# One sample tile of an input projection, dealt over four column groups of the matmul array

## The chip, the cores and the metric

The kernel runs on one core of one Trainium2 chip. The metric is the device time of one execution in microseconds (us). Three timed runs of the kernel before have a median of 1442.5 us.

## The reference, cut to what matters

One step of a streaming encoder layer, for a prompt of 1024 positions and a sample of 32 positions that follow a cache of 1024. Both go through the same weights. What the change touches is the first product, the normalised input times one wide weight matrix whose columns are split among the users:

```
PROJ_SIZES = (ATTN_WIDTH, ATTN_WIDTH, ATTN_WIDTH, N_IDX_HEADS * IDX_DIM, IDX_DIM, N_IDX_HEADS, SGU_WIDTH, SGU_WIDTH)
...
xn = _rms_norm(x, g_attn)
q, k, v, qi, ki, wi, u, vs = _mixer_inputs(xn, w_in, pos)      # jnp.split(xn @ w_in, ...), rotary on q, k, qi, ki
# qi, ki, wi: index scores, the 256 best keys of each query;  q, k, v: attention over those keys
# vs: gelu, normalised over groups of 128, mixed over 128 positions;  u: gelu, times the mixed vs
h = x + concat(attention, u * mixed) @ w_out
y = h + (silu(hn @ w_gate) * (hn @ w_up)) @ w_down
```

D_MODEL is 1024. The widths are 512, but for ki (64) and wi (8).

## The kernel before, in words

The 1056 rows are cut into nine tiles of 128, t = 0 to 8. Tile 8 (LAST) is the sample: its 32 rows (DEC) stand in the tile four times (PACK), loaded by four DMAs, so that all later steps find 128 rows. The matrix w_in is taken in seven chunks of columns, c = 0 to 6: qi, ki (with wi, 72 columns), vs, u, k, v, q, in this order. Every chunk but ki has 512 columns. The loop is over chunks, inside it over tiles, and each engine has its own written order for it (the function `step` in each engine's block); semaphores tie the orders together.

A float32 product is made of f16 parts: input and weight are each split into a high and a low part, and three products are summed (high x high, high x low, low x high). For one tile of one chunk, `main` on TensorE (L901, matmuls at L913) runs KT = 8 blocks of the 1024 times these three, 24 matmuls of up to 512 columns with a 128 x 128 stationary operand, into PSUM bank 2 or 3 (`par(c, t)` alternates).

What follows for each tile:

- ScalarE, `E` (L1279): empties the bank into the buffer e32 (for v: into r32 and V; for vs: through a Gelu with sums, four instructions at L1295).
- GpSimd, `A` (L705): rotary (L731 to L736) or, for u, a multiplication (L716), into r32. `B` (L738): subtraction that makes the low half (L763). In a tile's step GpSimd does A of this tile and then B of the tile before. For vs it has `vs_means` (L779), `vs_stats` (L768 to L774) and `vs_affine` (L784, L786).
- ScalarE, `H` (L1333, for vs L1314): cast to f16, the high half. `vs_squares` (L1362) and `vs_normalise` (L1371) for vs.
- TensorE, `post` (L946, L950): transposes of the two halves, called turns below, 8 at a time, two tiles late. In q there are two sets of turns a tile, the second after `dup_q` on ScalarE (L1347).
- ScalarE, `R` (L1392): empties the turns, two tiles late; `ST` (L1411): issues the store of k, v and ki rows.

A tile's `main` may start when E of two tiles before is done. ScalarE also splits the next chunk's weights (`piece_hi`, L436) in steps 0 and 1 of a chunk. From chunk u on, each step also holds one round of a binary search for the 256th best score: VectorE counts five score tiles (L1815), ScalarE two (`sign_count`, L1451, and L1455), VectorE judges (L1821) and sets the next bit (L1827). VectorE has 31 such rounds; the last is in tile 3 of q. Before that, in vs, the index scores are made (TensorE L972, ScalarE L1422, VectorE L1778 and L1781). After q, attention begins (TensorE L1039, VectorE L1923), then the output projection and the feed-forward.

In the output projection the sample's tile is already dealt over four column groups (L1138): each group of 32 columns of the array gets two of the eight blocks, and VectorE adds the four parts.

Of the kernel before, what the change touches and what calls it, by code (L numbers as in the profile page):

```python
# [36 lines left out]
P = 128  # L37
# [63 lines left out]
def encoder_step(nc, a):  # L101

    ctx = ExitStack()
    with ctx:
        M = ctx.enter_context(nc.sbuf_tensor("M", [P, 209600 // 4], F32))

        def sem(name):
            return ctx.enter_context(nc.semaphore(name))
# [120 lines left out]
        PS = ctx.enter_context(nc.psum_tensor("PS", [P, 8, 512], F32))  # L229
        PSf = PS[:, :, :].rearrange("p a b -> p (a b)")  # L230
        sign_out = view(RS, 8192, [TOK], F16)
        kth = cand.bitcast(F32)

        def bank(b):
# [19 lines left out]
        ws_turned, ws_hi, ws_lo, ws_ready = sem("ws_turned"), sem("ws_hi"), sem("ws_lo"), sem("ws_ready")  # L254
        kic_hi, kic_ready = sem("kic_hi"), sem("kic_ready")
        main_done, evac_done = sem("main_done"), sem("evac_done")
        rope_mul, r_ready = sem("rope_mul"), sem("r_ready")
        cast_done, sub_done, dup_done = sem("cast_done"), sem("sub_done"), sem("dup_done")
        post_done, post_evac = sem("post_done"), sem("post_evac")
# [60 lines left out]
            return FIRST_UNITS + before(c, lambda n: UNITS[n]) + UNITS[NAMES[c]] * t  # L320

        cC = {n: i for i, n in enumerate(NAMES)}

        def par(c, t):
            return (c + t) % 2
# [339 lines left out]
        def _(pool):  # L665
# [23 lines left out]

            x_rms(0, 0)  # L690
            x_rms(1, 1)
            pool.dma_start(ws32, a["w_s"][0].rearrange("g i j -> i g j")).then_inc(ws_loaded, 16)

            pool.wait_ge(kic_hi, 1)
# [194 lines left out]
        def _(pe):  # L889
# [11 lines left out]
            def main(c, t, rep):  # L901
                w = CHUNKS[c][2]
                b = 2 + par(c, rep)
                if c == 0:
                    pe.wait_ge(x_lo, t + 1)
                if c or not isinstance(t, int) or t >= 2:
                    pe.wait_ge(evac_done, n_step(c, t) - 1)
                for k in range(KT):
                    if isinstance(t, int) and t == 0 and k % pieces[first_piece[c]][2] == 0:
                        pe.wait_ge(w_split, first_piece[c] + k // pieces[first_piece[c]][2] + 1)  # L910
                    terms = ((0, wh), (0, wl), (1, wh))
                    for i, (s, wt) in enumerate(terms):
                        last = pe.matmul(bank(b)[:, 0:w], xnT[:, ds(t, 1), k, s, :].squeeze(1),  # L913
                                         wt[wbuf(c)][:, k * w:(k + 1) * w],
                                         start=(k == 0 and i == 0), stop=(k == KT - 1 and i == 2))
                last.then_inc(main_done, 1)

            def spatial(c, t, rep):
                pe.wait_ge(sub_done, n_cast(cC["vs"], t) + 1)
# [62 lines left out]
            for c in range(NC):  # L982
                def step(t, rep, c=c):
                    if c == 0 and isinstance(t, int) and t == 0:
                        main(c, t, rep)
                        X(1, 1)
                        return
                    if c == 0 and t_below(t, rep, LAST):
                        X(t + 1, rep + 1)
                    if c == 0 and isinstance(t, int) and t == 1:  # L990

                        pe.wait_ge(kic_ready, 1)
                        for s in range(2):
                            for i in range(8):
                                last = pe.transpose(bank16(4 + s)[:, i, :], dump[s][:, i * P:(i + 1) * P],
                                                    ident16[:])
                            last.then_inc(post_done, 1)
                        pe.wait_ge(ws_loaded, 16)
                        for g in range(GROUPS):
                            last = pe.transpose(bank(7)[:, g * P:(g + 1) * P], ws32[:, g, :], ident[:])  # L1000
                        last.then_inc(ws_turned, 1)
                    if NAMES[c] == "u":
                        if isinstance(t, int) and t == 0:
                            pe.wait_ge(ws_ready, 1)
                            pe.wait_ge(score_relu, NS * HEADS)
                        spatial(c, t, rep)
                    main(c, t, rep)
                    if NAMES[c] == "vs":
                        if t == 0:
                            flush(post, c - 1, 2)  # L1010
                        if t < NS:
                            score_products(t)
                    else:
                        lagged(post, c, t, rep, 2)
                steps(pe, c, step, *(LOOP[c] if c != 1 else (NT, NT)))
            flush(post, NC - 1, 2)

# [239 lines left out]
        def _(act):  # L1257
# [18 lines left out]
            act.wait_ge(kic_loaded, 16)  # L1276
            act.activation(kic2[0], kic32.unsqueeze(2).broadcast_to([P, 8, 2, HD]), ACT.Copy).then_inc(kic_hi, 1)

            def E(c, t, rep):  # L1279

                name, w, p = NAMES[c], CHUNKS[c][2], par(c, rep)
# [175 lines left out]
            for c in range(NC):  # L1457
                def step(t, rep, c=c):
                    if c == 0:
                        if t_below(t, rep, LAST):  # L1460
                            x_cast(t + 1, rep + 1)
                        if t_below(t, rep, LAST - 1):
                            x_square(t + 2, rep)
                    if NAMES[c] != "vs":
                        next_pieces(c, t)
                    lagged(dup_q, c, t, rep, 2)
                    E(c, t, rep)
                    if searching(c, t):
                        sign_count(c, t, 0)
                    if NAMES[c] == "vs":  # L1470
                        if t < NS:
                            score_relus(t)
                        vs_squares(c, t, rep)
                        next_pieces(c, t)
                    lagged(only_vs(H), c, t, rep, 2)
                    lagged(only_vs(ST), c, t, rep, 2)
                    lagged(only_vs(vs_normalise), c, t, rep, 1)
                    lagged(not_vs(H), c, t, rep, 1)
                    lagged(not_vs(ST), c, t, rep, 1)
                    if NAMES[c] == "u":  # L1480
                        sgu_evac(c, t, rep)
                    if isinstance(t, int) and t == 1 and NAMES[c] == "k":
                        act.wait_ge(score_acc, 2 * NS * HEADS)
                    lagged(R, c, t, rep, 2)
                    if searching(c, t):
                        sign_count(c, t, 1)
                    if c == 0 and isinstance(t, int) and t == 1:
                        for s in range(2):
                            act.wait_ge(post_done, s + 1)
                            act.activation(kiTs[:, s, :], PS[:, 4 + s, :].bitcast(F16),  # L1490
                                           ACT.Copy).then_inc(post_evac, 1)
                        act.wait_ge(ws_turned, 1)
                        act.activation(wmT[:, 0], bank(7).rearrange("p (g n) -> p g n", g=GROUPS), ACT.Copy,
                                       scale=WS).then_inc(ws_hi, 1)
# [724 lines left out]
```

## Time and profile before

| what | value |
|---|---|
| median of three runs (1441.97 to 1443.82) | 1442.5 us |
| the profiled execution | 1444.24 us |
| its span, first to last instruction | 1442.4 us |
| TensorE matmul busy | 1288.1 us (89%) |
| VectorE busy | 811.7 us (56%) |
| ScalarE busy | 716.7 us (50%) |
| GpSimd busy | 495.9 us (34%) |
| mean granted TensorE clock | 0.958 |

The times of instructions are from one profiled execution. Its span is counted from the first instruction, and all instants below are microseconds from there. TensorE is PE in the rows, its weight loads PEld, VectorE DVE, ScalarE ACT, GpSimd POOL. A row of a timeline has the start, the length, the engine, the line, the operation, what it writes and reads, and in brackets how long the engine had been idle before and what released it. TensorE's matmuls overlap, so a run of them is shorter than their number times the length of one. A granted clock of 1.00 is 2.4 GHz, 0.50 is 1.2 GHz.

### The profile page before, as it was taken

What the parts mean: (1) busy time and instruction counts of PE and PEld (TensorE: products, weight loads), DVE (VectorE), ACT (ScalarE), POOL (GpSimd) and SP (SyncE); (2) the same over time, 40 slices, a digit from 0 to 9 for tenths busy, and PEclk for the clock granted to TensorE, in tenths of its full rate; (3) what the DMA queues carried; (4) which work ended last, traced back from release to release, by engine and by line L of the source; (5) the groups of instructions that cost most, each with busy time, mean ns of one, the idle gap of its engine ahead of it and who ended that gap; (6) DMA issues with size and microseconds to landing.
All of it is one profiled execution on the core that took longest, in us unless ns stands there. A gap on an engine that the chain in (4) does not pass through costs nothing.

```text
span 1442.4 us, 29500 instructions
## 1 busy us (share of the span) xinstructions
PE 1288.1 (89%) x10636; PEld 927.3 (64%) x10636; DVE 811.7 (56%) x1495; ACT 716.7 (50%) x1408; POOL 495.9 (34%) x543
## 2 busy tenths in 40 slices
PE   4977788999996676798997999999999998999997
PEld 2443333544443445565455888888888887888886
DVE  4323675889889575896656555566555552212022
ACT  4546888787784844893434444444444441001011
POOL 4772436368258531442003333333333300000001
PEclk9989999999999579999998999999999999999999
DMA  6221001212100310114231222112222137211013
GB/s 196 89 61 35 15 1 46 59 37 82 65 17 0 87 38 16 45 31 140 88 103 41 63 58 58 43 45 58 58 58 58 29 90 206 62 63 37 0 30 91
DMA packets 81596, 86.69 MB, mean 60 GB/s; under 512 B 6768, under 2 KB 63120, under 8 KB 81520
## 3 DMA queue, kind: packets, MB, share of 16 engines
q1 hardware_dynamic: 76112, 75.07, 18.2%
q10 hardware_dynamic: 4848, 8.99, 1.7%
q0 software_dynamic: 560, 1.61, 0.4%
q8 instruction: 49, 0.80, 0.2%
q14 instruction: 27, 0.22, 0.0%
HBM read 72.34 MB, written 13.31 MB: 59 GB/s over the span
## 4 chain that ended last, share of the span: by engine, by line
PE 54%; DVE 5%; ACT 4%; issue 2%; POOL 2%; DMA 1%; SPq 1%; POOLq 0%; ACTq 0%; DVEq 0%
PE PS L1182 29%; PE PS L1239 15%; PE PS L1145 5%; DVE M L1934 1%; PE PS L1062 1%; PE PS L1039 1%; PE PS L1092 1%; DVE M L1923 1%; DMA M<-in_w_down 1%; ACT M L1524 1%; ACT M L1513 1%; SPq L647 1%; PE PS L1226 1%; PE PS L1159 0%; DMA M<-in_g_ffn 0%
## 5 line engine op out<-in xcount | busy, mean ns | idle before, releaser
L1182 PE MATMUL PS<-M 128*128 128x264 f16 x3696 | 420.8, 278 | 9.6 <-ACT M L1628 9.6
L1182 PEld LDWEIGHTS PS<-M 128*128 128x128 f16 x3696 | 363.3, 98 | 66.5 <-ACT M L1628 10.2
L913 PE MATMUL PS<-M 128*128 128x512 f16 (+1 forms) x1512 | 305.8, 363 | 3.6 <-DVE M L442 3.6
L1239 PE MATMUL PS<-M 128*128 128x256 f16 x2112 | 233.3, 274 | 6.3 <-DVE M L2148 6.3
L913 PEld LDWEIGHTS PS<-M 128*128 128x128 f16 (+1 forms) x1512 | 138.5, 103 | 153.9 <-issue 13.6
L1239 PEld LDWEIGHTS PS<-M 128*128 (+1 forms) x2112 | 207.2, 98 | 32.1 <-issue 7.3
L1815 DVE TENSOR_SCALAR_CACHE_REDUCE M<-M,small 128x384 f16<-128x384 f32 (+5 forms) x162 | 132.9, 881 | 0.8
L861 POOL TENSOR_TENSOR M<-M 128x264 f32<-128x264 f32 x44 | 34.7, 790 | 283.2 <-ACT M L1628 283.2
L683 POOL TENSOR_TENSOR small<-small 128x1 f32<-128x1 f32 x27 | 5.5, 203 | 331.5 <-ACT M L1720 237.2
L1987 DVE SCALAR_TENSOR_TENSOR M<-M 128x2048 f16<-128x2048 f32 (+1 forms) x44 | 88.9, 2025 | 36.1 <-ACT M L1566 36.1
L2148 DVE SCALAR_TENSOR_TENSOR M<-PS,M 128x256 f32 (+1 forms) x32 | 13.6, 424 | 165.5 <-PE PS L1239 165.4
L1628 ACT ACTIVATE M<-PS 128x264 f32<-128x264 f32 x132 | 51.2, 388 | 100.8 <-PE PS L1182 87.8
L1145 PE MATMUL PS<-M 128*128 128x512 f16 x384 | 84.2, 379 | 0.0
L1651 ACT ACTIVATE M<-M 128x1024 f16<-128x1024 f32 (+1 forms) x24 | 22.7, 978 | 116.8 <-PE PS L1226 82.3
L1451 ACT ACTIVATE M<-M,small 128x1056 f16<-128x1056 f32 x62 | 72.8, 1175 | 9.8 <-DVE small L1827 8.9
L1566 ACT ACTIVATE M<-M 128x2048 f16<-128x2048 f32 (+1 forms) x44 | 74.2, 1688 | 0.1
L1638 ACT ACTIVATE M<-M 128x264 f32 (+1 forms) x88 | 37.2, 423 | 70.2 <-DVE M L2072 36.2
L1062 PE MATMUL PS<-ident,M 128*128 128x128 f32 x306 | 56.5, 297 | 16.8 <-DVE M L1934 10.3
L1934 DVE TENSOR_TENSOR M<-PS,M 128x512 f16<-128x512 f32 (+3 forms) x102 | 53.4, 548 | 29.4 <-ACT M L1524 28.7
L2064 DVE TENSOR_TENSOR M<-PS,M 128x264 f32<-128x264 f32 x44 | 18.9, 431 | 83.8 <-PE PS L1182 82.3
L1145 PEld LDWEIGHTS PS<-M 128*128 128x128 f16 x384 | 37.5, 98 | 43.5
L1524 ACT ACTIVATE M<-PS 128x512 f16<-128x512 f32 (+3 forms) x102 | 47.9, 486 | 31.8 <-PE PS L1062 20.0
(177 smaller groups left out, 1943.0 us busy)
## 6 DMA issues: line engine op xcount, KB each, us to landing
M<-in_w_in SPq DMA_DIRECT2D x24, 512.0 KB, 3.7
M<-in_w_gate SPq DMA_DIRECT2D x22, 512.0 KB, 4.1
M<-in_w_up SPq DMA_DIRECT2D x22, 512.0 KB, 5.2
M<-in_w_down SPq DMA_DIRECT2D x20, 512.0 KB, 4.1
M<-in_x_prompt SPq DMA_DIRECT2D x16, 512.0 KB, 4.8
M<-in_w_out SPq DMA_DIRECT2D x8, 512.0 KB, 3.9
h_scratch<-M ACTq DMA_DIRECT2D x8, 512.0 KB, 5.1
M<-h_scratch SPq DMA_DIRECT2D x16, 256.0 KB, 7.3
```

The lines of the kernel that those rows point to most:

```text
L913: last = pe.matmul(bank(b)[:, 0:w], xnT[:, ds(t, 1), k, s, :].squeeze(1), wt[wbuf(c)][:, k * w:(k + 1) * w], start=(k == 0 and i == 0), st ...
L1062: last = pe.transpose(bank(pt_bank(g))[:, i * P:(i + 1) * P], LP[j % 4][:, (b0 + i) * P:(b0 + i + 1) * P], ident[:])
L1145: last = pe.matmul(bank(2 * p + d), mixT[:, t, k, s, :], wt[d][:, k * 512:(k + 1) * 512], start=(k == 0 and i == 0), stop=(k == KT - 1 and ...
L1182: last = pe.matmul(o, wsp[x][:, zw, wb, k * P:(k + 1) * P], ablk[:, ab, za, k * HT + s * SC:k * HT + (s + 1) * SC], start=(name not in kep ...
L1239: last = pe.matmul(o[:, 0:256], cols[:, ds(m * SC + r * P, P)], wt[dc % 2][:, f, :], start=(f == 0 and i == 0), stop=(f == FT - 1 and i == 2))
L1451: act.activation(sign_out, scores[:, o:o + TOK], ACT.Sign, scale=-1.0, bias=kth[:, j:j + 1], accum_out=signs[:, i:i + 1]).then_inc(signs_s ...
L1524: act.activation(PTs[pv_count[g] % 3][:, 0, 0:x * P], bank(pt_bank(g))[:, 0:x * P], ACT.Copy).then_inc(pt_hi, 1)
L1566: act.activation(wsp[x][:, 0, 4 * half:7 if half else 4, :], tb if half else raw[x], ACT.Copy, scale=WS).then_inc(w2_hi, 1)
L1628: act.activation(buf[s], bank(BANKS[x][s]["a"])[:, 0:SC], ACT.Copy).then_inc(kept, 1)
L1815: dve.tensor_scalar(dump[x][:, 0:S], scores[:, o:o + S], kth[:, j:j + 1], None, ALU.is_ge, ALU.add, accum_out=cnt[:, j:j + 1]).then_inc(se ...
L1934: dve.tensor_tensor(r[:, 1, 0:x * P], bank(pt_bank(g))[:, 0:x * P], r[:, 0, 0:x * P], ALU.subtract).then_inc(pt_ready, 1)
L1987: dve.scalar_tensor_tensor(out=wsp[x][:, 1, b, :], in0=tb if half else raw[x], scalar=WS, in1=wsp[x][:, 0, b, :], op0=ALU.mult, op1=ALU.su ...
```

## The change

In the six chunks of 512 columns, tile 8 is no longer a full product. Each of the four column groups of the array gets 32 columns of the stationary operand (the sample's rows once) and two of the eight blocks, so that 24 matmuls of 128 x 32 by 512 leave four partial sums of the 32 rows in the four quarters of the bank's partitions. ScalarE copies the bank into e32 (r32 for v). One f32 matmul with a 128 x 128 matrix of zeros and ones (`fold`, four times four identities of 32 x 32) adds the four parts and writes the sum to all four quarters, into the same bank. E then empties it as before.

`fold` is made once by GpSimd, by four copies after the second tile's statistics, ahead of the load of w_s. On TensorE the f32 product stands after the turns of the step; in vs, where the step has none, directly after the dealt products. On ScalarE the copy takes E's old place in the step, and E stands at its end: after the turns' evacuation R, and in vs after the cast of tile 6.

```
+        def dealt(c, t):
+            return isinstance(t, int) and t == LAST and CHUNKS[c][2] == 512
...
             x_rms(1, 1)
+            pool.wait_ge(ident_ready, 1)
+            for i in range(PACK):
+                rows = slice(i * DEC, (i + 1) * DEC)
+                if i:
+                    pool.wait_ge(fold_ready, i)
+                pool.tensor_copy(fold[rows].rearrange("p (r n) -> p r n", r=PACK),
+                                 ident[rows, rows].unsqueeze(1).broadcast_to([DEC, PACK, DEC])).then_inc(fold_ready, 1)
+            pool.wait_ge(fold_ready, PACK)
...
+                if dealt(c, t):
+                    for n in range(6):
+                        for j in range(PACK):
+                            k, i = 2 * j + n // 3, n % 3
+                            s, wt = ((0, wh), (0, wl), (1, wh))[i]
+                            last = pe.matmul(bank(b)[j * DEC:(j + 1) * DEC, :], xnT[:, t, k, s, 0:DEC],
+                                             wt[wbuf(c)][:, k * w:(k + 1) * w], start=(n == 0), stop=(n == 5))
+                    last.then_inc(parts_done, 1)
+                    return
...
+            def fold_parts(c):
+                p = par(c, LAST)
+                if c == 0:
+                    pe.wait_ge(fold_ready, PACK)
+                pe.wait_ge(parts_kept, n_dealt(c) + 1)
+                pe.matmul(bank(2 + p), fold, (r32 if NAMES[c] == "v" else e32)[p], start=True,
+                          stop=True).then_inc(main_done, 1)
...
                         lagged(post, c, t, rep, 2)
+                    if dealt(c, t):
+                        fold_parts(c)
...
+            def keep_parts(c):
+                p = par(c, LAST)
+                act.wait_ge(parts_done, n_dealt(c) + 1)
+                if NAMES[c] == "v":
+                    wait_r_free(act, c, LAST, p)
+                else:
+                    wait_e_free(act, c, LAST)
+                act.activation((r32 if NAMES[c] == "v" else e32)[p], bank(2 + p), ACT.Copy).then_inc(parts_kept, 1)
...
-                    E(c, t, rep)
+                    if dealt(c, t):
+                        keep_parts(c)
+                    else:
+                        E(c, t, rep)
                     if searching(c, t):
                         sign_count(c, t, 0)
                     if NAMES[c] == "vs":
                         if t < NS:
                             score_relus(t)
-                        vs_squares(c, t, rep)
+                        if not dealt(c, t):
+                            vs_squares(c, t, rep)
                         next_pieces(c, t)
                     lagged(only_vs(H), c, t, rep, 2)
                     lagged(only_vs(ST), c, t, rep, 2)
+                    if NAMES[c] == "vs" and dealt(c, t):
+                        E(c, t, rep)
+                        vs_squares(c, t, rep)
                     lagged(only_vs(vs_normalise), c, t, rep, 1)
...
                     lagged(R, c, t, rep, 2)
+                    if dealt(c, t) and NAMES[c] != "vs":
+                        E(c, t, rep)
```

## Rows read from the trace of the kernel before

**Rows 1.** Busy us (instructions) by stretch; PEclk is TensorE's granted clock.
```profile
core 0: us, PE busy (x) PEld busy (x) DVE busy (x) ACT busy (x) POOL busy (x), PEclk, DMA share, GB/s
...
350.60:404.50 53.90, 53.67 (x263) 24.66 (x261) 49.37 (x119) 43.64 (x78) 18.18 (x15) 1.00 0.17 60
...
253.00:255.10 2.10, 2.05 (x20) 2.06 (x21) 2.06 (x6) 1.86 (x4) 0.00 (x0) 0.52 0.00 0
...
244.00:250.50 6.50, 6.45 (x26) 2.55 (x24) 5.54 (x12) 5.70 (x12) 2.62 (x3) 0.83 0.05 13
```
**Rows 2.** Timeline of all engines, end of qi; start us, us, engine, line, operation, releaser.
```profile
88.13 0.60 ACT L1303 ACTIVATE M<-PS 128x512 f32<-128x512 f32 x1 [3.60 <-PE PS L913]
88.32 0.62 PE L950 MATMUL PS<-ident,M 128*128 128x128 f16 x8 [0.23 <-POOL M L763]
...
88.80 1.27 POOL L731 TENSOR_TENSOR M<-M 128x512 f32<-128x512 f32 x1 [0.54 <-ACT M L1303]
89.14 1.01 ACT L1392 ACTIVATE M<-PS 128x1024 f16<-128x1024 f16 x1
```
**Rows 3.** Timeline of all engines, end of u and first tile of k.
```profile
291.80 1.16 POOL L763 TENSOR_TENSOR M<-M 128x512 f16<-128x512 f32 x1
...
293.61 0.60 ACT L1298 ACTIVATE M<-PS 128x512 f32<-128x512 f32 x1 [0.90 <-PE PS L913]
...
301.01 0.58 ACT L1303 ACTIVATE M<-PS 128x512 f32<-128x512 f32 x1
```
**Rows 4.** Timeline of all engines, end of k and first tiles of v.
```profile
348.90 1.16 POOL L763 TENSOR_TENSOR M<-M 128x512 f16<-128x512 f32 x1
...
350.31 0.60 ACT L1303 ACTIVATE M<-PS 128x512 f32<-128x512 f32 x1 [1.55 <-PE PS L913]
...
356.68 0.58 ACT L1288 ACTIVATE M<-PS 128x512 f32<-128x512 f32 x1
...
368.07 0.23 DVE L1821 TENSOR_SCALAR small<-small 128x7 uint32<-128x7 f32 x1 [1.70 <-ACT small L1455]
```
**Rows 5.** Timeline of all engines, end of vs.
```profile
228.29 0.28 ACT L1295 ACTIVATE M<-PS 128x128 f32<-128x128 f32 x1
...
231.85 0.20 POOL L779 TENSOR_TENSOR small<-small 128x4 f32<-128x4 f32 x1
232.08 0.40 ACT L1362 ACTIVATE M<-M,small 128x128 f32<-128x128 f32 x1 [2.65 <-POOL small L779]
```
**Rows 6.** Timeline of all engines, end of v and first tiles of q.
```profile
400.61 0.60 ACT L1288 ACTIVATE M<-PS 128x512 f32<-128x512 f32 x1 [0.69 <-DMA out_v_p<-M]
...
404.55 0.58 ACT L1303 ACTIVATE M<-PS 128x512 f32<-128x512 f32 x1
...
412.58 1.18 ACT L1451 ACTIVATE M<-M,small 128x1056 f16<-128x1056 f32 x1 [2.08 <-DVE small L1827]
```
**Rows 7.** Timeline of all engines, end of q and attention's first score.
```profile
460.32 0.58 ACT L1303 ACTIVATE M<-PS 128x512 f32<-128x512 f32 x1
...
460.97 2.23 POOL L731 TENSOR_TENSOR M<-M 128x512 f32<-128x512 f32 x1 [1.22 <-ACT M L1303]
461.74 1.93 ACT L1392 ACTIVATE M<-PS 128x1024 f16<-128x1024 f16 x2
...
479.08 0.29 DVE L1923 CUSTOM_DVE_ANT_0 M<-PS,cmask 128x128 f32<-128x128 f32 x1 [12.67 <-PE PS L1039]
```
**Rows 8.** TensorE's timeline, at four places of the kernel.
```profile
39.08 1.04 PE L898 MATMUL PS<-ident,M 128*128 128x128 f32 x8
...
253.05 1.03 PE L946 MATMUL PS<-ident,M 128*128 128x128 f16 x8 [2.60 <-POOL M L763]
...
662.14 2.77 PE L1138 MATMUL PS<-M 128*32 128x512 f16 x48
...
665.30 10.52 PE L1145 MATMUL PS<-M 128*128 128x512 f16 x48
```
**Rows 9.** All matmuls of line 913; nanoseconds minimum, median and maximum.
```profile
L913 PE MATMUL PS<-M x1512: 196/379/634, 15.6 to 458.1; 128*128 128x512 f16 x162, 128*128 128x72 f16 x27
```
**Rows 10.** GpSimd's timeline after the loads that it issues.
```profile
26.68 0.18 POOL L683 TENSOR_TENSOR small<-small 128x1 f32<-128x1 f32 x1 [2.74 <-ACT M L1263]
```

More of the change, by code:

```diff
@@ L231, in encoder_step @@
         sign_out = view(RS, 8192, [TOK], F16)
+        fold = view(RS, 8192 + 2 * TOK, [P], F32)
         kth = cand.bitcast(F32)
@@ L256, in encoder_step @@
         main_done, evac_done = sem("main_done"), sem("evac_done")
+        fold_ready, parts_done, parts_kept = sem("fold_ready"), sem("parts_done"), sem("parts_kept")
         rope_mul, r_ready = sem("rope_mul"), sem("r_ready")
@@ L322, in encoder_step, with n_dealt @@
         cC = {n: i for i, n in enumerate(NAMES)}
+        def dealt(c, t):
+            return isinstance(t, int) and t == LAST and CHUNKS[c][2] == 512
+        def n_dealt(c):
+            return sum(CHUNKS[x][2] == 512 for x in range(c))
         def par(c, t):
```

## The prediction, made before the changed kernel was run

> **What bounds the kernel now.** I read the profile in this order. First the busy time by stretch, to find where the changed work lies: the input projection runs from 10 to 478 us, and in the stretch that holds chunk "v" TensorE is busy nearly all the time while VectorE and ScalarE are not far behind [rows 1]. So there TensorE looks like the bound, and elsewhere nothing looks like it alone. A share of busy time doesn't say which wait ends last, so I then went to the timeline of each engine at the six tiles that the change touches (tile 8 of chunks qi, vs, u, k, v and q), and read at the evacuation of that tile (called E below, on ScalarE) how long it had waited for TensorE. It waited 3.60 us in qi [rows 2], 0.90 in u [rows 3] and 1.55 in k [rows 4]. In vs it starts right behind other ScalarE work [rows 5], in v it waited 0.69 us for a store to land and not for TensorE [rows 6], in q it starts behind other ScalarE work too [rows 7]. That is the whole of what an earlier product could give at these places: 3.60 + 0.90 + 1.55 = 6.05 us, and in qi GpSimd, which needs E next, had waited only 0.54 us [rows 2]. So the most that can come back is about 0.5 + 0.9 + 1.55 = 3 us. TensorE's own saving is far larger, and most of it has nobody waiting for it.
>
> **What is removed.** A full product of one tile is 24 matmuls of 512 columns, half of the 48 that take 10.52 us: 5.3 us. The same number dealt over four column groups is half of 2.77: 1.4 us [rows 8]. So TensorE is freed of 3.9 us at each of six tiles, 23 us in all.
>
> **What is added, at each of the six.** (1) A ScalarE copy of 128x512 out of PSUM, by the row of E itself 0.60 us [rows 2]. (2) One f32 product of 512 columns, which the trace doesn't show. From below: f32 transposes of 8 x 128 = 1024 columns took 1.04 us, so 0.5 us for 512 [rows 8]. From above: four f16 passes, 4 x 0.22 (5.3 / 24) = 0.9 us, and at the low clock, where one product's record grows from 379 to 634 ns [rows 9], 4 x (0.22 + 0.255) = 1.9 us. I take 0.9 at full clock and 1.7 at the low one, since a full f32 product is nearer to a real f16 product than to a transpose. The Trainium skill's FP8 and Floating Point Precision (TensorE Precision Notes) says that true f32 takes four passes through the array; by it the price would be the 0.9 that I took. (3) The order. On TensorE the f32 product stands behind the turns (8 transposes) of tile 6, and these wait for GpSimd's subtraction; behind it stands the next chunk's first product. On ScalarE E moves behind a sign count, the cast of tile 7, the issue of tile 7's store and the evacuation of tile 6's turns (R). GpSimd's rotary work, statistics or multiplication for tile 8 waits for E, and behind it on GpSimd waits the subtraction of tile 7, for which TensorE's next turns wait. The store of tile 7 is issued about as before. SP's queue gets nothing new.
>
> (4) GpSimd builds the 0/1 matrix: four small copies ahead of the w_s load and six other issues of its queue. They cost between 4 x 0.18, a one-column operation [rows 10], and 4 x 0.32, a quarter of the 1.27 us that 512 columns take [rows 2]: 0.7 to 1.3 us. The w_s load and the six issues behind them on its queue start later by that. GpSimd idles 2.74 us before its work at 26.68, so I take nothing; without that cover it would be the 1.3 us.
>
> **The clock.** After 2.60 us of idle TensorE came back with a granted clock of 0.52, the 1.2 GHz level, and 8 turns took 1.03 instead of 0.62 us; a 24-matmul product begun that way took about 6.45 us with a mean clock of 0.83 [rows 1, 8]. The change opens an idle stretch of 3 to 6 us between the dealt products and the turns or the copy at each of the six. So I expect the low clock at most of them: turns 0.4 longer, the f32 product 0.8, the next chunk's first product up to 1.1.
>
> **Place by place**, as a shift of what comes next.
>
> qi: the dealt products end near 84.2 (3.9 before 88.13). The turns of tile 6 can't start before 88.32 [rows 2], so they end at 88.9 to 89.4; R takes 1.01, the f32 product 0.5 to 1.9 beside it. E starts at 90.0 to 91.2 instead of 88.13: +1.9 to +3.1. GpSimd follows, then the turns of tile 7, chunk ki and the first score product, with no slack that I find. I take +2.5.
>
> vs: E stood at 228.29, ahead of the cast of tile 6. Now it stands behind it, and the cast waits for GpSimd's work that ends at 231.85; 0.6 for the cast and 4 x 0.28 for E give 233.6, and GpSimd's mean, then at 231.85, waits for E. The squares at 232.08 had waited for that mean [rows 5]. +1.9, or 1.5 if reads overlap better.
>
> u: the 0.90 wait goes, 0.60 comes: -0.3. But the next product starts after subtraction (292.96), turns and f32 product, at 294.1 to 295.9, and lasts 5.3 to 6.5: until 299.4 to 302.4. Its evacuation stood at 301.01 [rows 3]. So -0.3 to +1.4; I take +0.5.
>
> k: the same. At best 1.55 - 0.60 = 0.95 is won. The turns wait until 350.06, the next product ends between 356.5 and 359.5, and its evacuation stood at 356.68 [rows 4]. VectorE's search round waits for that chain (1.70 us at 368.07), so a delay reaches it: -0.9 to +2.5. E itself falls from 350.31 behind R, and GpSimd's next turns with it; I take +1.8.
>
> v: no turns stand before the f32 product, but the copy inherits E's wait for the store: 400.61 + 0.6, then f32 product until 401.7 to 403.1, then 5.3 to 6.5 us: E of q's first tile at 407.0 to 409.6 instead of 404.55. ScalarE waited 2.08 us for VectorE soon after, at 412.58 [rows 6], which hides part: 0 to +3.3. I take +1.2.
>
> q: E, cast and two R ended at 463.67. The copy takes E's place and E follows them: 463.7 instead of 460.32, +3.4. GpSimd's first operation there took 2.23 us beside VectorE's mask work, against 1.27 in qi; begun later, it and the next ones meet less of that, and up to 1.9 comes back. VectorE then waits 12.67 us for attention's first product at 479.08 [rows 7], so nothing hides the rest: +1.5 to +3.4. I take +2.0.
>
> Sum: 2.5 + 1.9 + 0.5 + 1.8 + 1.2 + 2.0 = +9.9 us; low ends +3.7, high ends +15.6. After attention's start nothing depends on an absolute time, so it stays to the end. The profiled execution took 1444.24 us (1.84 beside its span of 1442.4), 1.7 above the median of 1442.5; the shift is the same on either, and on the median it gives 1452.4.
>
> The Trainium skill's TensorEngine Tiling (PSUM Bottleneck) warns that dealing products over groups speeds TensorE and not the emptying of PSUM. The wait rows agree for vs, v and q; by it alone (six copies of 0.60 and no other delay) the time would be 1446.1, at the lower edge of the forecast below; it has no chance of its own.
>
> **Rivals.** The saving lands (1440, chance 0.06). Mechanism: E comes earlier than before in qi, u and k, and 3 us come back. For it: the three waits above. Against it: the turns that stand before E. It decides from the point where GpSimd has freed the turns of tile 6 before the dealt products end; in k these end near 346.4 (350.31 less 3.9) and GpSimd frees the turns at 350.06 [rows 4], so it would have to be 3.7 us earlier. 1442.5 - 3 = 1439.5 to 1440.
>
> It is absorbed (1443 to 1445, chance 0.14). The search on VectorE takes up what k and v lose, the clock stays full, u and k win 1.2 us together, and only qi, vs and part of q remain, less what the ki chunk and the scores take up: 0.5 to 2.9 us. For it: ScalarE waited 2.08 us for VectorE at 412.58 [rows 6], so VectorE sets the pace there. Against it: nothing that I find covers vs and q.
>
> Everything adds (1456 to 1458, chance 0.2). One mechanism, the low clock at all six: each f32 product at 1.9 us and each next product 1.1 us longer, which brings every place to its high end but for part of q. It decides where the gap before the f32 product is as long as the 2.60 us after which the clock had fallen [rows 1, 8]. 1442.5 + 14 to 15.6.
>
> The forecast as worked out, between these (1446 to 1456): 0.6.
>
> About 0.2% (2.9 us) is what can be told from no change. Faster 0.06, same 0.14, slower 0.8. For eight in ten I take 1444 to 1458, which leaves out the first rival, about half of the second and little of the third.
>
> **What would show it.** Right: a dealt group of 24 in 1.4 to 1.6 us; E of tile 8, against the work before it, 2 to 3 us later in qi, 4 in vs and 3 in q; first score product 2 to 3 us late; first attention product 8 to 12 us late; the f32 product in 0.9 to 1.9 us with a clock of 0.5 before it. Wrong: the clock stays at 1.0 in these gaps, or attention starts within 3 us of 478.5.

## The result and the profile after

| | before | after |
|---|---|---|
| median, on one chip | 1442.24 us (1441.67 to 1443.82) | 1456.87 us (1453.67 to 1459.30) |
| runs | 4 | 4 |
| profiled execution, its span | 1444.24, 1442.4 us | 1455.27, 1453.4 us |
| mean granted TensorE clock | 0.958 | 0.956 |

The ratio on record is 1.0085, 95% interval [1.0071, 1.0099]: slower by 0.7 to 1.0%. The two medians lie 14.6 us apart, a ratio of 1.0101, just above that interval; why the two figures differ isn't known, so the loss is told here as 10 to 15 us. The forecast was 1452.4 with a range of 1444 to 1458; the median lies inside, near the upper end.

**Where the 11 us of the span arise.** Single executions of one kernel differ by some us in stretches that nothing has changed, so I don't compare instants of two traces but six distances inside each trace, one around every place: qi, GpSimd's first rotary operation of tile 7 to that of tile 8; vs, `vs_means` of tile 7 to tile 8; u, from there to the rotary operation of k's tile 0; k, from there to that of k's tile 8; v, from there to that of q's tile 7; q, from there to the table load with which ScalarE enters attention. The price of a place is its distance less that of before. All are in the table of the experiments; for the change they are 2.78, 1.80, 0.23, 2.67, 3.00 and 0.97, together 11.45 us.

How one comes about, at k. GpSimd's rotary operations of tiles 7 and 8, before:

```profile
344.94 1.28 POOL L731 TENSOR_TENSOR M<-M 128x512 f32<-128x512 f32 x1 [0.59 <-ACT M L1303]
...
350.99 1.28 POOL L731 TENSOR_TENSOR M<-M 128x512 f32<-128x512 f32 x1 [0.92 <-ACT M L1303]
```

And all engines at the end of k, after (L929 the dealt products, L1321 the copy, L983 the turns, L948 the f32 product, L1347 E, L779 the subtraction, L1332 E of v's tile 0):

```profile
350.73 1.28 POOL L747 TENSOR_TENSOR M<-M 128x512 f32<-128x512 f32 x1 [0.57 <-ACT M L1347]
350.83 1.48 PE L929 MATMUL PS<-M 128*32 128x512 f16 x24
...
354.57 0.60 ACT L1321 ACTIVATE M<-PS 128x512 f32<-128x512 f32 x1
...
355.88 1.03 PE L983 MATMUL PS<-ident,M 128*128 128x128 f16 x8 [3.57 <-POOL M L779]
356.71 2.02 PE L948 MATMUL PS<-M 128*128 128x512 f32 x2
...
358.77 0.60 ACT L1347 ACTIVATE M<-PS 128x512 f32<-128x512 f32 x1
...
359.44 1.27 POOL L747 TENSOR_TENSOR M<-M 128x512 f32<-128x512 f32 x1 [3.62 <-ACT M L1347]
...
363.39 1.16 POOL L779 TENSOR_TENSOR M<-M 128x512 f16<-128x512 f32 x1
364.72 0.60 ACT L1332 ACTIVATE M<-PS 128x512 f32<-128x512 f32 x1 [2.08 <-POOL M L779]
```

The distance between the rotary operations is 8.71 us against 6.05 before: +2.66. E begins 4.2 us after the copy. In GpSimd's step the subtraction of tile 7 stands behind the rotary work of tile 8, which waits for E; so that subtraction, too, ends only at 364.5, and E of v's first tile, which writes the buffer r32 that it reads, waits 2.08 us for it. Before, it waited for nothing [rows 4]. So a late E reaches v through GpSimd's order and a buffer. TensorE is close behind: v's first product, begun late at 358.52, ends at 364.21, 0.3 us before that subtraction. That GpSimd's path does it alone is shown by the last experiment.

The end of qi, of u and of v, after (L938 is `main`, L979 the turns of u):

```profile
83.70 1.48 PE L929 MATMUL PS<-M 128*32 128x512 f16 x24
85.28 0.60 ACT L1321 ACTIVATE M<-PS 128x512 f32<-128x512 f32 x1
...
89.18 0.72 PE L983 MATMUL PS<-ident,M 128*128 128x128 f16 x8 [4.00 <-POOL M L779]
89.70 2.02 PE L948 MATMUL PS<-M 128*128 128x512 f32 x2
...
91.75 0.60 ACT L1347 ACTIVATE M<-PS 128x512 f32<-128x512 f32 x1 [0.79 <-PE PS L948]
...
299.11 0.62 PE L979 MATMUL PS<-ident,M 128*128 128x128 f16 x8 [3.30 <-POOL M L779]
299.57 1.08 PE L948 MATMUL PS<-M 128*128 128x512 f32 x2
...
401.87 1.48 PE L929 MATMUL PS<-M 128*32 128x512 f16 x24
...
408.14 0.60 ACT L1321 ACTIVATE M<-PS 128x512 f32<-128x512 f32 x1
408.79 2.07 PE L948 MATMUL PS<-M 128*128 128x512 f32 x2 [5.45 <-ACT M L1321]
410.66 17.27 PE L938 MATMUL PS<-M 128*128 128x512 f16 x72
...
417.61 0.60 ACT L1347 ACTIVATE M<-PS 128x512 f32<-128x512 f32 x1 [3.95 <-PE PS L938]
...
422.79 0.60 ACT L1347 ACTIVATE M<-PS 128x512 f32<-128x512 f32 x1 [1.89 <-PE PS L938]
```

In qi the copy is done at 85.9, but the f32 product stands behind turns that GpSimd frees at 89.1. In v nothing stands before the f32 product but the copy, and ScalarE comes to that 4.8 us after the dealt products' end. TensorE, which ran ahead of ScalarE in v, now waits 5.45 us for it, and then q's first three products take 17.27 us at a lower clock. ScalarE waits 3.95 and 1.89 us for them, where the first had found its product ready [rows 6]. The clock by windows, after:

```profile
core 0: us, PE busy (x) PEld busy (x) DVE busy (x) ACT busy (x) POOL busy (x), PEclk, DMA share, GB/s
...
89.20:92.00 2.80, 2.80 (x18) 1.58 (x19) 0.00 (x0) 1.27 (x2) 0.00 (x0) 0.56 0.00 0
...
408.70:428.00 19.30, 19.21 (x79) 8.35 (x80) 16.28 (x40) 10.92 (x21) 9.54 (x10) 0.87 0.06 19
429.80:435.00 5.20, 5.20 (x29) 2.37 (x27) 2.92 (x8) 5.17 (x8) 4.78 (x5) 1.00 0.02 5
```

0.56 in the turns and the f32 product of qi, little above the 1.2 GHz level, where the f32 product takes 2.02 us; at full clock, in u, it takes 1.08.

Vs and q, after (L1358 the cast of tile 6, L1406 the squares of tile 8):

```profile
232.04 0.60 ACT L1321 ACTIVATE M<-PS 128x512 f32<-128x512 f32 x1
232.69 2.07 PE L948 MATMUL PS<-M 128*128 128x512 f32 x2 [6.91 <-ACT M L1321]
...
235.66 0.63 ACT L1358 ACTIVATE M<-M 128x512 f16<-128x512 f32 x1 [3.02 <-POOL M L802]
...
237.63 0.40 ACT L1406 ACTIVATE M<-M,small 128x128 f32<-128x128 f32 x1 [0.31 <-POOL small L795]
...
474.99 0.61 ACT L1347 ACTIVATE M<-PS 128x512 f32<-128x512 f32 x1
475.68 1.26 POOL L747 TENSOR_TENSOR M<-M 128x512 f32<-128x512 f32 x1 [4.48 <-ACT M L1347]
...
477.89 0.71 POOL L749 TENSOR_TENSOR M<-M 128x256 f32<-128x256 f32 x1
...
490.90 1.28 ACT L1566 ACT_TABLE_LOAD   x1
```

The squares come 1.97 us after the cast. In q, E is 3.2 us later against its surroundings than before (474.99 for 460.32, where the tile before it is 11.45 late), but GpSimd's operations are shorter again than in [rows 7] (1.26 for 2.23), and 0.97 is left.

**Ahead of the places and behind them.** GpSimd's build at the start, and what follows it:

```profile
17.12 3.94 POOL L705 COPY M<-ident 32x128 f32<-32x128 f32 x4
...
27.04 0.20 POOL L691 TENSOR_TENSOR small<-small 128x1 f32<-128x1 f32 x1
...
27.90 2.28 DVE L1783 SCALAR_TENSOR_TENSOR M<-M,small 128x1024 f32<-128x1024 f32 x1 [1.02 <-POOL small L693]
...
30.24 1.97 PE L914 MATMUL PS<-ident,M 128*128 128x128 f32 x8 [5.67 <-DVE M L1783]
```

3.94 us, where 0.7 to 1.3 was estimated. GpSimd's wait of 2.74 us [rows 10] is gone, its statistics of tile 2 come 0.36 us later (27.04 for 26.68), and VectorE's normalisation of that tile runs beside GpSimd's rotary work and takes 2.28 us, where other tiles take 1.28. From tile 1 to tile 7 of qi this execution is 0.85 us late.

After attention's start (+12.42) the lateness isn't constant: it is 14.29 us where the transfer of g_ffn for the output projection is issued, 12.54 where VectorE begins the step that waits for it, and 11.0 at the end, 1.4 less than at attention's start. First VectorE's row of before, then that of after:

```profile
668.50 3.72 DVE L2001 SCALAR_TENSOR_TENSOR M<-PS,M 32x1024 f32<-32x1024 f32 x3 [1.95 <-DMA M<-in_g_ffn]
```

```profile
681.04 3.71 DVE L2054 SCALAR_TENSOR_TENSOR M<-PS,M 32x1024 f32<-32x1024 f32 x3 [0.19 <-DMA M<-in_g_ffn]
```

VectorE had waited 1.95 us for it and now waits 0.19, because the transfer landed 4.07 us after its issue instead of 5.83. So the wait gives back about what attention had lost, and the 1.4 us come behind it. None of this can be put down to the change: in the eleven other kernels below the transfer takes 4.1 to 6.2 us, attention's start comes 182.9 to 187.6 us ahead of its issue, and from VectorE's step to the end it is 771.6 to 774.4 us.

### The profile page after: what moved, and what is told of

Its sections match the earlier page's. It is cut to its first block, busy times and chain, and to the rows that moved or that the text cites. A ratio compares the mean times of both kernels' runs of the same rounds, so it can differ in the third digit from the quotient of the medians.

```text
span 1453.4 us, 29541 instructions
## 1 busy us (share of the span) xinstructions
PE 1275.8 (88%) x10648; PEld 919.4 (63%) x10648; DVE 812.6 (56%) x1495; ACT 719.8 (50%) x1414; POOL 498.3 (34%) x547
## 4 chain that ended last, share of the span: by engine, by line
PE 54%; DVE 5%; ACT 4%; issue 2%; POOL 2%; DMA 1%; SPq 1%; POOLq 0%; ACTq 0%; DVEq 0%
PE PS L1217 28%; PE PS L1274 15%; PE PS L1180 6%; DVE M L1987 1%; PE PS L1097 1%; PE PS L1074 1%; PE PS L1127 1%; DVE M L1976 1%; ACT M L1577 1%; DMA M<-in_w_down 1%; ACT M L1566 1%; SPq L655 1%; PE PS L1261 1%; PE PS L1194 0%; PE PS L1094 0%
## 5 line engine op out<-in xcount | busy, mean ns | idle before, releaser
L938 PE MATMUL PS<-M 128*128 128x512 f16 (+1 forms) x1368 | 275.4, 363 | 3.6 <-DVE M L450 3.6
L938 PEld LDWEIGHTS PS<-M 128*128 128x128 f16 (+1 forms) x1368 | 125.6, 104 | 142.4 <-issue 18.9
L983 PE MATMUL PS<-ident,M 128*128 128x128 f16 x306 | 28.1, 240 | 44.3 <-POOL M L779 23.5
```

## The experiments

Two theories. **Order**: the loss is the place of E and of the f32 product in the engines' orders. **Work**: it is the added work itself, the copies, the f32 products and the low clock. Later a third, **coupling**: TensorE, which ran ahead of ScalarE, has to wait for a copy that ScalarE makes late.

Prices of the places in us, from each trace as defined above, and the timed ratio to the kernel before on the same chip:

| kernel | qi | vs | u | k | v | q | sum | ratio, 95% interval |
|---|---|---|---|---|---|---|---|---|
| the change | 2.78 | 1.80 | 0.23 | 2.67 | 3.00 | 0.97 | 11.5 | 1.0085 [1.0071, 1.0099] |
| build alone | 0.00 | 0.0 | 0.0 | 0.0 | 0.1 | 0.0 | 0.1 | 1.0016 [1.0006, 1.0026] |
| build later | 2.67 | 1.80 | 0.62 | 2.68 | 2.85 | 0.96 | 11.6 | 1.0086 [1.0071, 1.0102] |
| early f32 product and E | -0.38 | 0.42 | 1.53 | 0.53 | 3.00 | 0.87 | 6.0 | 1.0058 [1.0043, 1.0074] |
| order alone | 1.79 | 1.82 | 0.20 | 2.68 | -0.57 | 0.86 | 6.8 | 1.0056 [1.0042, 1.0071] |
| f32 product behind next | 3.08 | 1.81 | -0.09 | 2.67 | -0.02 | 0.97 | 8.4 | 1.0062 [1.0042, 1.0083] |
| clock held | 1.78 | 1.79 | 0.46 | 2.65 | 0.49 | 0.99 | 8.2 | 1.0076 [1.0057, 1.0095] |
| v alone | 0.0 | 0.0 | 0.1 | 0.0 | 0.19 | 0.0 | 0.3 | 1.0010 [0.9996, 1.0024] |
| k and v | 0.0 | 0.0 | -0.1 | 6.52 | 0.23 | -0.23 | 6.4 | 1.0066 [1.0042, 1.0090] |
| six, placed | -0.39 | 0.42 | 0.31 | 0.31 | 0.41 | 0.98 | 2.0 | 1.0010 [0.9998, 1.0022] |
| qi, u, v, placed | -0.38 | 0.0 | 0.5 | 0.0 | 0.0 | 0.0 | 0.2 | 1.0009 [0.9996, 1.0022] |
| k's order alone | 0.0 | 0.0 | 0.0 | 2.67 | -0.67 | 0.0 | 2.0 | 1.0033 [1.0019, 1.0047] |

0.0010 is 1.4 us. In places that an experiment leaves as they were before, the prices are within 0.25 of 0 but for v (-0.67 with k's order alone), which takes up part of what k loses. Where an experiment keeps the change's own edit they differ by more: qi 2.67 to 3.08, u -0.09 to 0.62. A row of prices is that of one profiled execution, and that can be a short one: 1448.86 for the order alone, whose median is 1452.91, and 1449.63 for the f32 product behind next, whose median is 1453.46. So the sum of a row needn't be the timed difference.

**Build alone.** The kernel before with the four copies after `x_rms(1, 1)`.

> The kernel before, with GpSimd's four copies that build the 0/1 matrix at their place of the change, and nothing else; the matrix isn't used. Theory A (the build isn't hidden: in the changed kernel's trace it takes 3.94 us of GpSimd, and the sixth product of chunk qi already starts 0.85 us late, long before the first dealt tile): slower by 0.86 us, 0.5 to 1.2. Theory B (the build is hidden by GpSimd's waits, and the 0.85 us has another cause): within 0.3 us of the kernel before.

Median 1446.24 against 1444.17: slower by 0.9 to 3.8 us. Theory A holds in sign; the size is not settled, see the next.

**Build later.** The change with the same copies in step 1 of chunk qi on GpSimd.

> The whole change, with the build of the 0/1 matrix moved into GpSimd's wait of 5.61 us ahead of the rotary work of tile 1 (behind the statistics of tile 3). Theory A: the 0.86 us come back and nothing else moves: 1456.0 against the 1456.9 of the change, 13.7 us over the kernel before. Theory B (not the build): 1456.9, no difference from the change.

1456.24; the ratio is that of the change. The copies, there:

```profile
35.17 2.21 POOL L806 COPY M<-ident 32x128 f32<-32x128 f32 x4
```

2.21 us for the same four copies that took 3.94 at their first place, where VectorE splits weights at the same time. One by one they took 1.13, 1.17, 1.17 and 0.29 us there, and 0.28, 1.17, 0.29 and 0.29 here. The four long ones started while VectorE was inside an operation on 128 x 1024, and each ended 0.14 to 0.15 us after it; the four short ones didn't. It is the same in all ten traces with the build. A gain of 0.86 can't be told within this interval, and none is seen. By tile 1 this trace is 1.02 us early against before and that of the change 0.86 late, but the kernel with the order alone, which has no build and is the kernel before until tile 7, is 1.67 early there. So single traces vary by more than the term in question. All traces together say a little more: at tile 1 the five with the build at its first place are 0.11 to 1.33 us late against before, the eight others, before among them, between 1.67 early and 0.59 late, and the means differ by 1.2 us. That the build costs is shown by the timing of it alone; how much of the change's loss it is stays open, with about 1 us as the likely size.

**Early f32 product and E.**

```
                     last.then_inc(parts_done, 1)
+                    fold_parts(c)
                     return
...
                     if dealt(c, t):
                         keep_parts(c)
-                    else:
-                        E(c, t, rep)
+                    E(c, t, rep)
```

> The whole change, but with the f32 product directly behind the dealt products on TensorE and the evacuation E directly behind the copy on ScalarE, at its old place. Theory A (the place in the order carries the loss: f32 product behind the turns, E behind a sign count, a cast and the turns' evacuation): the dealt product, copy and f32 product take 1.5 + 0.6 + 1.1 = 3.2 us against 5.3, so E comes up to 2.1 us earlier where it waits for TensorE; by place qi -0.5, vs +1.1, u -0.4, k -1.0, v -1.5, q +1.2, build +0.9: within 3 us of the kernel before, 1439 to 1445. Theory B (the added work itself carries it: copies, f32 products at the low clock): most of the change's 14.6 us stays, 1450 or more.

1452.48: Theory B by the number (1450 or more), but not by place. At qi, vs and k the order was the loss (-0.38, 0.42, 0.53 for 2.78, 1.80, 2.67). At v nothing changed: there the f32 product already stood behind the dealt ones, and the 5.45 us of wait for ScalarE are still there. At u it is worse by 1.3 than in the change; there the f32 product follows 3.67 us of idle TensorE and ran at a granted clock of 0.61, and in the change at 1.00. The wait at v is where the theory of coupling comes from.

**Order alone.** Full products; `if not dealt(c, t): E(c, t, rep)` at the old place, E at the change's place.

> The kernel before with E of tile 8 moved to the place that the change gives it on ScalarE; full products, no copy, no f32 product, no build. Theory A (the place in the order carries the loss): in qi E starts behind the turns' evacuation, at 90.1 for 88.1, +2.0; vs +1, k +1, v +0.5, q +1.5, u 0: +6 (4 to 8), 1448. Theory B (the added work carries it): within 2 us of the kernel before.

1452.91, 8.7 us more than before by the medians, a little above Theory A's 4 to 8. By place it is Theory A: vs, u, k and q cost what they cost in the change, with no dealt product, no copy and no f32 product in the kernel. What it doesn't explain is v, where a late E alone costs nothing, and 1.0 of qi's 2.78.

**F32 product behind the next chunk's first product**, in vs and v.

```
                     main(c, t, rep)
+                    if c and isinstance(t, int) and t == 0 and NAMES[c - 1] in FOLD_LATE:
+                        fold_parts(c - 1)
```

> The whole change, but in chunks vs and v the f32 product stands behind the next chunk's first product on TensorE (E waits for it at its place of the change). Theory W (the loss is TensorE's wait for the copy, which ScalarE comes to late: 6.91 us idle ahead of the f32 product in vs, 5.45 us in v): the next chunk's first product, 5.3 us, fills that wait, the f32 product starts as now, and chunk q gets up to 5 us earlier, of which v's +3.0 comes back; with the low clock of u's body (0.6): 3 to 6 us less than the change, 1451 to 1454. Theory L (the loss at v is that E itself is late on ScalarE): within 1 us of the change.

1453.46; v falls from 3.00 to -0.02, and the interval overlaps that of the change. At v, filling the wait takes the whole price away. But two things went with the wait: TensorE's idle time and the low clock behind it, for the f32 product now takes 1.12 us at a granted clock of 1.00, where the change's took 2.07 at 0.50. The next run tells them apart. At vs the same wait was filled and nothing changed (1.81): there nobody waits for TensorE.

**Clock held.** Products into a bank that nothing reads, in TensorE's waits.

> The whole change, with idle products into an unused bank on TensorE (14 in qi, k and v behind the dealt products, 18 in q between the two turns), 0.22 us each, so that its waits of 3.6 to 5.5 us shrink below 2.5 us and the clock stays up; nothing waits for these products but TensorE's own queue. Theory C (the low clock is a large part of the loss): f32 product 1.08 for 2.02 us and turns 0.62 for 1.03 at qi, k and q, f32 product at v: 1.35 x 3 + 0.9 = 5 us at most, 3 to 5 us less than the change, 1452 to 1454. Theory W (the waits themselves carry it, and what follows the f32 product isn't near TensorE's bound): 0 to 1.5 us less.

TensorE at the end of qi and of v (L945 the idle products, L952 the f32 product):

```profile
84.53 3.19 PE L945 MATMUL PS<-M 128*128 128x512 f16 x14
88.61 0.62 PE L989 MATMUL PS<-ident,M 128*128 128x128 f16 x8 [0.88 <-POOL M L779]
89.07 1.08 PE L952 MATMUL PS<-M 128*128 128x512 f32 x2
...
403.96 3.19 PE L945 MATMUL PS<-M 128*128 128x512 f16 x14
407.73 1.12 PE L952 MATMUL PS<-M 128*128 128x512 f32 x2 [0.57 <-ACT M L1329]
408.69 15.70 PE L938 MATMUL PS<-M 128*128 128x512 f16 x72
```

The clock stays up: the f32 product takes 1.08 for 2.02 in qi and 1.12 for 2.07 in v, q's three first products 15.70 for 17.27. That takes 1.0 from qi and 2.5 from v, and nothing from k and q. In v the two savings, 0.95 and 1.57, add up to the 2.5. There q's first product still stands behind the f32 product, so TensorE's lost lead by itself is worth no more than the 0.49 that is left; the rest of v was the low clock behind the wait. The prices fall by 3.3 us together, within Theory C's 3 to 5 but not at its places; the timing (1455.72, +10.8 against before) allows for it and doesn't show it, its interval meets that of the change.

**V alone**: only v dealt, f32 product behind q's first product, E directly behind the copy, build later.

> Only chunk v is dealt, its f32 product stands behind q's first product, E directly behind the copy, and the matrix is built in GpSimd's wait ahead of the rotary work of tile 1. Theory W: TensorE is the bound in v, so q's first product starts 3.9 us earlier and its E follows v's E at once, 2 us earlier than before: 2 us less than the kernel before (0.5 to 3.5). Theory S (ScalarE and VectorE set the pace of q anyway, so TensorE's saving has nobody waiting for it even here): from 0.5 us less to 1 us more than before.

No gain: 1446.95 against 1444.88, from 0.6 us less to 3.5 more. Theory S, though not for its reason alone: q's first product starts at 397.98, 5.35 us long, but its E comes at 408.09, because E of v stands before it on ScalarE and had waited for the f32 product until 404.41; then ScalarE waits for VectorE as before (2.09 us at 415.45).

**K and v.**

> As the kernel with v alone, and chunk k dealt too, its f32 product behind v's first product and its E at the change's place on ScalarE (behind the turns' evacuation). Theory W: v's products start 3.9 us earlier and stay so to the end of v, less 0.9 for the f32 product: 3 us on top of v alone, 4 us less than the kernel before (2 to 6). Theory S: no gain over v alone, and up to 1 us lost by E's lateness in k.

No gain, as Theory S said, but a loss far beyond its 1 us: k 6.52. Its f32 product, moved behind v's first product, brings E, GpSimd's subtraction of tile 7 and with it the buffer for v's first E later still. What helps at v harms at k. The ten timed runs spread from 1448.49 to 1461.07, and the four of about 1460 have a mean granted clock of 0.946 to 0.947, the six others 0.951 to 0.956; why is not found.

**All six, each at the place that the runs above point to**, with every copy and f32 product of the change: early in qi, vs and k, the change's order in u and q, behind the next chunk's first product in v.

> All six chunks dealt as in the change, the same copies, f32 products and matrix; only places differ: in qi, vs and k the f32 product directly behind the dealt products and E directly behind the copy; u and q as in the change; in v the f32 product behind q's first product; the build in GpSimd's wait ahead of the rotary work of tile 1. Theory P (the loss is the sum of places, each as the traces of the earlier runs show it: qi -0.4, vs +0.4, u -0.3 and +0.5 in its body, k +0.5, v 0, q +0.9): 1 to 2 us more than the kernel before, some 12 us less than the change. Theory X (places aren't additive, a gain at one is lost at the next): 5 us or more over before.

1445.81 against 1444.76. Theory P: the prices are 2.0 together, and the ratio holds 1. The end of v in it (L1341 E of v, L1356 E of q, L1504 a sign count):

```profile
395.72 5.35 PE L945 MATMUL PS<-M 128*128 128x512 f16 x24 [0.65 <-ACT M L1342]
...
400.92 1.13 PE L955 MATMUL PS<-M 128*128 128x512 f32 x2
...
403.34 0.58 ACT L1341 ACTIVATE M<-PS 128x512 f32<-128x512 f32 x1
...
405.70 0.58 ACT L1356 ACTIVATE M<-PS 128x512 f32<-128x512 f32 x1
...
408.36 1.18 ACT L1504 ACTIVATE M<-M,small 128x1056 f16<-128x1056 f32 x1 [2.08 <-DVE small L1889]
```

TensorE's longest wait here is 2.41 us, behind the f32 product, and ScalarE waits for VectorE's search as in [rows 6]. This kernel also has the build at its later place, so its gain over the change is that of the places and of the build together.

**Qi, u and v, placed**: the version that the traces pointed to as the fastest.

> Only qi, u and v dealt, each at its best place seen (qi: E behind the copy, u: as in the change, v: f32 product behind q's first product), late build: the version that the traces point to as the fastest. Theory P: qi -0.4, u -0.3 (+0.5 in its body), v 0: 0 to 0.8 us less than the kernel before, which the timing can hardly tell from none. Rival: 1.5 us or more to either side, by a coupling that the places alone don't show.

1445.99 against 1444.76, from 0.6 us less to 3.2 more: no gain is seen, and the rival isn't excluded. No version that beats the kernel before was found.

**K's order alone**: the kernel before, E of k's tile 8 behind R.

> The kernel before, with nothing but E of tile 8 of chunk k moved behind the turns' evacuation (its place in the change); full product, no copy, no f32 product. Theory A (at k E's place in ScalarE's order is the whole loss: rotary work of tile 8 late, so GpSimd's subtraction, so the buffer that v's first E waits for): rotary work of k's tile 8 comes 2.7 us later against that of tile 7 than before, and v starts so much later; 2.5 us slower, 1 to 4. Theory B (the f32 product behind the turns is needed for the loss): within 1 us of before.

1448.79 against 1444.76, slower by 2.7 to 6.8 us, where 1 to 4 was expected. GpSimd and ScalarE:

```profile
345.60 1.28 POOL L731 TENSOR_TENSOR M<-M 128x512 f32<-128x512 f32 x1 [0.57 <-ACT M L1303]
...
354.30 1.27 POOL L731 TENSOR_TENSOR M<-M 128x512 f32<-128x512 f32 x1 [3.58 <-ACT M L1303]
...
358.25 1.15 POOL L763 TENSOR_TENSOR M<-M 128x512 f16<-128x512 f32 x1
359.57 0.60 ACT L1288 ACTIVATE M<-PS 128x512 f32<-128x512 f32 x1 [2.07 <-POOL M L763]
```

Theory A: the same distance of 8.70 us between the rotary operations, the same wait of 2.07 us for the buffer, and nothing of the change in the kernel but the place of one instruction.

## Why the prediction was right, and where its terms were off

**That TensorE's saving has no taker** was right. At the six places 23 us of TensorE's products are gone (the f32 products take 10 of them back in the change), and the kernel with all six in good places is not faster. The Trainium skill's TensorEngine Tiling (Array Packing), section PSUM Bottleneck, says that dealing speeds the products and not the emptying of PSUM. The traces agree: E takes 0.60 us as before, the copy 0.60 more, and v alone freed 3.9 us of TensorE and won nothing.

**The costs of the parts** were right: a dealt group 1.48 (1.4 to 1.6 forecast), the copy 0.60, the f32 product 1.08 and 2.02 to 2.07 in its records, 0.91 and about 1.85 until the next instruction starts (0.9 and 1.7 to 1.9).

**Place by place**, forecast against price: qi 2.5 and 2.78, vs 1.9 and 1.80, u 0.5 and 0.23; these steps held, and the order alone reproduces vs and u. In qi the order alone gives 1.79, and the clock held shows 1.0 as the clock's. The others were mis-sized:

- k, +1.8 against 2.67. The step looked for the loss in the next product on TensorE, its turns and its clock. The order alone and the clock held show that neither matters: it is E behind R, through GpSimd's order and the buffer r32. The sentence that E falls behind R was there; its price wasn't worked out.
- v, +1.2 against 3.00. The step let ScalarE's wait of 2.08 us for VectorE hide part of the delay. That cover lies behind two waits of ScalarE for TensorE now, and it hid none. The clock held shows 2.5 us as the clock's: that of the f32 product and of three products behind it, where the step had one. What the step didn't name is the long wait that brings this clock: ScalarE comes late to the copy, and TensorE stands idle 5.45 us ahead of the f32 product, with q's first product behind it in its order. With that product in front, both the wait and the price are gone.
- q, +2.0 against 0.97. GpSimd gets back 2.3 of the 3.26 us by which its first rotary operation is late (14.71 against 11.45 for the tile before): 12.42 at attention's start. The prediction allowed for 1.9 of that and took less.

The sum was 9.9 for 11.45, and that it came so near is partly luck: k and v were taken 2.7 us too low, q 1.0 too high. One term outside it was wrong. The build, taken as nothing, took three times the upper end of its estimate. The estimate of one copy was right where VectorE was not inside an operation (0.28 to 0.29 for at most 0.32); the others took 1.13 to 1.17, each until just after VectorE's operation, which the step didn't consider. That the shift stays to the end after attention's start is neither shown nor refuted: it was 12.42 us there and 11.0 at the end, and the kernels differ by as much in those stretches.

One row was misread. The product of 6.45 us [rows 1], from which the up to 1.1 us of a next product comes, began after TensorE had been idle for 5.22 us, not 2.60; the product that followed the 2.60 took 6.01, 0.7 us more than at full clock. Of the signs named beforehand, E of tile 8 was 2.8 us late in qi, 4.2 in vs and 3.2 in q against the work before it, as said; attention's first product was 12.42 late, a little over the 8 to 12.

**The rivals.** The median lies just above the 1446 to 1456 of the forecast as worked out. "Everything adds" by the low clock at all six would have given 1456 to 1458, and 1456.87 lies there; but its mechanism fell. The clock was low at five of the six, and holding it up where it was tried gave 1.0 and 2.5 us at qi and v and nothing at k and q. That the saving lands, or that VectorE's search absorbs the loss, is refuted for this order of work; in the kernel with all six in good places the time is that of the second, and ScalarE waits for VectorE's search as before.

Open: the size of the build's price, why the ratio and the medians differ, the spread of the runs of the kernel with k and v, and why single traces differ by up to 3 us in the ki chunk and the first scores, where the kernels with the build alone and with v alone lose 2.8 and 3.1 us that the change doesn't.

## What to carry to other kernels

Before a step is split in two, look at who stands between the halves in each engine's written order: here one instruction moved behind others in ScalarE's order cost as much at k (2.67 us) as the whole change there. An engine that runs ahead stands idle when its next instruction needs an answer from the engine behind it, and TensorE then came back at a low clock; put the next independent product in between, but only where nobody waits for the answer (at v it took 3 us away, 2.5 of them the clock's; at k it cost 4 more). And a saving on the busiest engine counts only where a wait for it ends last.

## What the runs showed of the hardware

- An f32 product of 512 columns takes 0.91 us to the next start at full clock, 4.1 times the 0.22 of an f16 product of the same columns, and twice that at the low level.
- TensorE came back at full clock from an idle stretch of 3.30 us in u (turns 0.62) and at about half from one of 3.57 in k (turns 1.03), but also from one of 2.60 in the kernel before [rows 8]; the length of the idle stretch alone doesn't tell.
- With 14 to 18 products into an unused bank in TensorE's waits, the f32 products of qi, k, v and q ran at a granted clock of 1.00 (1.08 to 1.13 us); without them at 0.50 (2.02 to 2.07). No place's price rose by more than 0.23 us.
- A GpSimd copy of 32 partitions x 128 f32 took 0.28 to 0.29 us by itself. One that started inside a VectorE operation on 128 x 1024 (1.2 to 1.3 us) took 1.13 to 1.17 and ended 0.14 to 0.15 us after it, in all ten traces with the build.
